# Two transformer blocks in one launch: a merged set of edits, and TensorE multiplying the identity while it waits for a norm

## The chip, the cores and the metric

The kernel runs on one core of a Trainium2 chip. A core has TensorE (matrix products into PSUM), VectorE, ScalarE, GpSimd and SyncE, which here issues all loads; 16 DMA engines move the data. The time is device time in microseconds (us) of the whole launch, median of several runs. In the profile PE is TensorE's matmuls, PEld its weight loads, DVE is VectorE, ACT ScalarE, POOL GpSimd, and SPq the queue of SyncE.

## What is computed

All is float32, with 256 tokens of width 1024. Cut to what matters:

```python
def first_block(x):                     # two layers
    for i in (0, 1):
        h = rms_norm(x, mix_pre_g[i])
        y = conformer_conv_module(h) if i == 0 else dilated_mixture_attention(h, k_sh, v_sh)
        x = x + rms_norm(y, mix_post_g[i])
        y = conv_ffn(rms_norm(x, ffn_pre_g[i]))          # 1024 -> 2 x 2816 -> 1024
        x = x + rms_norm(y, ffn_post_g[i])
        if i == 0:
            k_sh, v_sh = split(rms_norm(x, kv_norm_g) @ w_kv)
def second_block(x):
    u = modulate(rmsnorm(x, norm1_g), sh1, sc1)          # sh, sc, g from silu(c) @ ada_w
    x = x + g1 * token_mixer(u, uc)                      # mLSTM and differential attention
    u = modulate(rmsnorm(x, norm2_g), sh2, sc2)
    logits = u @ router_w + router_b                     # 32 experts, the best 4 of each token
    gate = softmax(top_k(logits, 4))
    y = sum over experts e of gate_e * (swiglu(u @ w1[e] + b1[e]) @ w2[e] + b2[e])
    x = x + g2 * y
    return rmsnorm(x, final_norm_g)
```

## The kernel before

**Layout.** Activations lie feature-major: eight chunks (`KT`) of 128 features by 256 tokens. Weights of the dense layers come in slabs of 1 MB (128 x 2048 floats) through a ring of five (`RING`), in the order of `LOADS`; slab `g` may be loaded when slab `g - 5` has been used (`slab_used`). SyncE issues them in one written-out order, and it also waits in that order, so that whatever stands behind a wait in its program is late with it.

**Dense stages.** `product` (L513) multiplies one slab by the eight chunks: 16 matmuls of 128x128 by 256, each two instructions in the trace, into one of three PSUM banks ("units"). `stage` (from `product`) runs the slabs of one matrix. The first product after a norm is the one with `wait_chunk`: it takes the chunks in the order in which the norm delivers them (L523); the others run at L534. A norm goes: ScalarE squares, TensorE multiplies by a constant mean matrix (`stat`, L574), ScalarE takes the root, VectorE the reciprocal, and VectorE or ScalarE scales the chunks. Before three of the products (`n2`, `n4`, `n7`) the norm's scale is applied later, so the product needs only the residual; the squares of these norms are summed by GpSimd (`presum`, L1306), and TensorE multiplies the sum (`presummed`, L590) after the first product. The residual is L1334 and L1337 of VectorE.

**Between the mixer and the experts.** SyncE stands at `wa`, the first matrix after attention, until the last head is done, and loads the router's weights and the experts' b2 into memory that attention used. After `wo` come the norm `n10`; 16 transposes of H into token-major `U2T` (L871); the router's products, 16 with 32 columns (L879); on VectorE the best four of each token in two passes, one for each half of the tokens (from L1685); products that count the tokens of each expert (L885 to L890); eight products of b2 and the gates (L900), copied to `YACC`; and `gather(0)` (L911), which picks the tokens of the first two experts.

**Experts.** A loop over 16 pairs of experts. Each pair has 24 slabs of 1 MB: 16 in `up` (L940 bias, L946), eight in `down` (L973). Within a pair stand also `scatter` (L922) of the pair before, which VectorE adds into `YACC` (L1770), the gather of the next pair (L911) and transposes (`hidden`). The slabs go round through 12 slots (`EXPERT_RING`): the five of the ring, three in `spare`, four in `arena`. Since 24 is a multiple of 12, one body serves every pair. A slab is loaded when the slab 12 places before it has been used (L503). The first five slots are loaded as the ring comes free, the other seven when the last product of `wo` is done. At the end stand one more scatter, X + g2 * YACC in eight operations (L1809), the last norm (L1015, L574, L1318, L1324) and one store of 1 MB (L507).

Of the kernel before, what the change touches and what calls it, by code (L numbers as in the profile page):

```python
# [19 lines left out]
P = 128  # L20
T = 256
D = 1024
KT = D // P
# [5 lines left out]
EXPERTS = 32  # L29
TOP_K = 4  # L30
CAP = 64
PAIRS = EXPERTS // 2
SLAB = 2048
RING = 5
EXPERT_RING = 12
# [151 lines left out]
def build(nc, d_x, d_ctx, d_par, d_con, d_mmask, d_rows, d_gatew, d_routerw, d_b1, d_b2, d_cond, d_dense, d_experts, d_out):  # L187
    ctx = ExitStack()
    with ctx:
# [6 lines left out]
        for kind, count, stages in (  # L196
                ("sq", KT, norms + ["hm", "do", "n10", "n11"]), ("sum", 1, norms + ["n10", "n11"]),
                ("root", 1, norms + ["n10", "n11"]), ("x", KT, ["n1", "n3", "n6", "n8", "n11"]),
# [105 lines left out]
        U2T = tiles(area(NB, 2048), 2)  # L304
        YACC = tiles(area(NB + 2048, 2048), KT)
        XGT = tiles(area(NB + 4096, 1024), KT)
        GL, LN, SGM = (tiles(area(NB + 5120 + 512 * i, 512), 2) for i in range(3))
        ACTT = tiles(area(NB + 6656, 1024), 8)
        YE = area(NB + 7680, 1024)
        SGT = area(NB + 8704, 256)  # L310
        SEL = tiles(area(NB + 8960, 256), 2)
        SELG = tiles(area(NB + 9216, 256), 2)
        NCOL = 4 * EXPERTS + 2
        POSA = tiles(area(NB + 9472, 2 * NCOL), 2)
        GATA = tiles(area(NB + 9472 + 2 * NCOL, 2 * NCOL), 2)
        MO = NB + 9472 + 4 * NCOL
# [4 lines left out]
        GTT = arena[0:EXPERTS, MO + 640:MO + 896]  # L321
        MORE = [spare[:, SLAB * i:SLAB * (i + 1)] for i in range(3)] + [area(NB + 11264 + SLAB * i, SLAB) for i in range(4)]
        B2 = arena[0:EXPERTS, NB + 19456:NB + 20480]
        ACTS = tiles(area(NB + 19456, 1024), 4)
# [14 lines left out]
        RW = area(NB + 20480, 256).rearrange("p (k n) -> p k n", k=KT)  # L339
# [4 lines left out]
        def expert_slab(j):  # L344

            q = j % EXPERT_RING
            return slab(DENSE_SLABS + q) if q < RING else MORE[q - RING]

        def slot_sem(j):
            q = j % EXPERT_RING  # L350
            return sem(f"slab{(DENSE_SLABS + q) % RING if q < RING else q}")
# [51 lines left out]
        def passes(eng, body, first=None):  # L403

            with eng.Fori(0 if first is None else first, PAIRS) as p:
                body(p)
            extra = extra_passes(eng)
            loaded[eng] = extra
            with eng.If(extra > 0):
                with eng.Fori(PAIRS, (extra + 1) * PAIRS) as n:  # L410
                    body(n)
# [38 lines left out]
        def _(sp):  # L450
# [3 lines left out]
            sp.dma_start(par[:, :], d_par).then_inc(sem("par_in"), 16)  # L454
            for g in range(DENSE_SLABS):
# [14 lines left out]
                if g == SLAB_AT["wa", 0]:  # L470
                    sp.wait_ge(sem("d_pv"), HEADS)
# [1408 lines left out]
```

## Time and profile before

| | |
|---|---|
| median of 3 runs | 2550.23 us (2549.61 to 2550.98) |
| the profiled execution, its own time | 2555.48 us |
| its span, first to last instruction | 2553.7 us |
| mean granted TensorE clock | 0.975 of full |
| PE busy, share | 2400.6 us, 94% |
| DVE, ACT, POOL busy | 752.9, 423.7, 17.0 us |
| read from HBM | 604.65 MB, 237 GB/s over the span |

Busy shares are averages over the span. The rows of slices show how they change: each digit is one fortieth of the span (63.8 us), in tenths of full. In brackets behind a row stands how long the engine had been idle before it, and what ended the idle time.

### The profile page before, as it was taken

How to read it: one execution, taken by the hardware profiler on the slowest of the kernel's cores; microseconds unless marked ns; L12 is line 12 of the kernel's file. 1: busy time of each engine (PE TensorE's matmuls, PEld its weight loads, DVE VectorE, ACT ScalarE, POOL GpSimd, SP SyncE). 2: the span in 40 equal slices, each digit the busy share in tenths (PEclk: the TensorE clock that was granted, in tenths of full speed). 3: DMA queues.
4: the chain of work that ended last, by engine and by line, in shares of the span. 5: the costliest groups of instructions: out<-in, count | busy, mean ns of one | idle time of the engine just before them, and what ended most of it. 6: DMA issues, size and time to landing. Idle time of an engine off the chain costs nothing.

```text
span 2553.7 us, 32904 instructions
## 1 busy us (share of the span) xinstructions
PE 2400.6 (94%) x13428; PEld 1806.2 (71%) x13428; DVE 752.9 (29%) x1781; ACT 423.7 (17%) x948; POOL 17.0 (1%) x25
## 2 busy tenths in 40 slices
PE   8799999999889998999998798999999999999997
PEld 7678888888778887888776586555555555555554
DVE  5834373210533312000345533222212211111212
ACT  3231102010331103000023512111111111111111
POOL 0000000000000000000000000000000000000000
PEclk9899999999999999899999997999999999999999
DMA  6134476654124443131120144999999999999996
GB/s 239 43 106 159 148 280 231 231 215 174 56 97 151 148 148 116 50 128 71 66 83 33 66 170 169 393 422 421 422 422 422 422 421 422 422 422 422 422 422 254
DMA packets 83841, 606.88 MB, mean 238 GB/s; under 512 B 9328, under 2 KB 9712, under 8 KB 10000
## 3 DMA queue, kind: packets, MB, share of 16 engines
q1 hardware_dynamic: 83760, 605.73, 59.9%
q8 instruction: 59, 0.97, 0.2%
q14 instruction: 22, 0.18, 0.0%
HBM read 604.65 MB, written 1.05 MB: 237 GB/s over the span
## 4 chain that ended last, share of the span: by engine, by line
PE 79%; DMA 10%; DVE 6%; ACT 3%; issue 1%; SPq 0%; ACTq 0%; DVEq 0%
PE bank L534 26%; PE bank L946 13%; DMA spare<-in_experts 9%; PE bank L531 8%; PE bank L973 6%; PE bank L605 5%; PE bank L523 4%; PE bank L911 3%; PE bank L548 2%; PE bank L940 2%; DVE arena L1436 2%; PE bank L922 1%; PE bank L685 1%; PE bank L616 1%; PE bank L574 1%
## 5 line engine op out<-in xcount | busy, mean ns | idle before, releaser
L534 PE MATMUL bank<-arena,ring 128*128 128x256 f32 x3296 | 717.2, 380 | 0.0
L534 PEld LDWEIGHTS bank<-arena,ring 128*128 128x128 f32 x3296 | 629.4, 191 | 84.4
L946 PE MATMUL bank<-ring,arena 128*64 128x256 f32 x2304 | 293.9, 383 | 18.2 <-DMA ring<-in_experts 10.3
L946 PEld LDWEIGHTS bank<-ring,arena 128*64 128x64 f32 x2304 | 175.2, 137 | 132.1 <-DMA ring<-in_experts 20.4
L1789 DVE TENSOR_SCALAR arena<-bank 128x256 f32<-128x256 f32 x64 | 27.2, 425 | 704.9 <-PE bank L946 704.9
L531 PE MATMUL bank<-ring,arena 128*128 128x256 f32 x896 | 196.1, 382 | 0.0
L531 PEld LDWEIGHTS bank<-ring,arena 128*128 128x128 f32 x896 | 171.7, 192 | 23.1
L946 PE MATMUL bank<-spare,arena 128*64 128x256 f32 x768 | 117.5, 383 | 7.9 <-DMA spare<-in_experts 7.9
L605 PE MATMUL bank<-arena,ring 128*128 128x256 f32 x576 | 124.6, 379 | 0.0
L523 PE MATMUL bank<-arena,ring 128*128 128x256 f32 x352 | 93.0, 431 | 29.2 <-ACT arena L1030 15.1
L605 PEld LDWEIGHTS bank<-arena,ring 128*128 128x128 f32 x576 | 109.7, 190 | 14.7
L946 PE MATMUL bank<-arena 128*64 128x256 f32 x1024 | 117.6, 383 | 0.0
L973 PE MATMUL bank<-spare,arena 128*64 128x512 f32 x384 | 113.3, 595 | 0.0
L973 PE MATMUL bank<-arena 128*64 128x512 f32 x512 | 113.1, 593 | 0.0
L523 PEld LDWEIGHTS bank<-arena,ring 128*128 128x128 f32 x352 | 76.8, 220 | 44.6 <-issue 31.8
L946 PEld LDWEIGHTS bank<-arena 128*64 128x64 f32 x1024 | 70.7, 137 | 44.6 <-issue 12.3
L1414 DVE SCALAR_TENSOR_TENSOR arena<-ring,arena 128x1024 f32<-128x1024 f32 x64 | 74.9, 1222 | 72.7 <-DMA ring<-in_dense 72.6
L946 PEld LDWEIGHTS bank<-spare,arena 128*64 128x64 f32 x768 | 69.2, 137 | 31.0 <-DMA spare<-in_experts 13.3
L1273 ACT ACTIVATE arena<-arena 128x256 f32<-128x256 f32 x64 | 26.7, 417 | 386.7 <-DVE arena L1789 377.7
L973 PEld LDWEIGHTS bank<-arena 128*64 128x64 f32 x512 | 44.2, 137 | 65.6 <-issue 65.6
L548 PE MATMUL bank<-arena,ring 128*128 128x256 f32 x384 | 88.9, 390 | 0.0
L1357 DVE SCALAR_TENSOR_TENSOR arena<-arena,par 128x254 f32<-128x254 f32 (+1 forms) x176 | 73.3, 479 | 51.0 <-ACT arena L1054 51.0
(260 smaller groups left out, 2146.3 us busy)
## 6 DMA issues: line engine op xcount, KB each, us to landing
ring<-in_dense SPq DMA_DIRECT2D x186, 1024.0 KB, 4.8
ring<-in_experts SPq DMA_DIRECT2D x160, 1024.0 KB, 22.4
arena<-in_experts SPq DMA_DIRECT2D x128, 1024.0 KB, 21.4
spare<-in_experts SPq DMA_DIRECT2D x96, 1024.0 KB, 21.8
con<-in_con SPq DMA_DIRECT2D x1, 1248.0 KB, 12.2
X<-in_x SPq DMA_DIRECT2D x1, 1024.0 KB, 5.0
arena<-in_cond SPq DMA_DIRECT2D x1, 1024.0 KB, 17.7
arena<-in_ctx SPq DMA_DIRECT2D x1, 1024.0 KB, 4.9
```

What stands on the lines that cost most here:

```text
L523: ins = nc.tensor.matmul(half_of(u, j), w[:, k, j * P:(j + 1) * P], src[:, k, :], start=(k == 0 and j == 0), stop=(k == KT - 1), skip_grou ...
L531: ins = nc.tensor.matmul(o, src[:, k, j * P:(j + 1) * P], w[:, k, :], start=(k == 0), stop=(k == KT - 1))
L534: ins = nc.tensor.matmul(o, w[:, k, j * P:(j + 1) * P], src[:, k, :], start=(k == 0), stop=(k == KT - 1))
L548: ins = nc.tensor.matmul(o, w[:, k, j * P:(j + 1) * P], H[:, k, :], start=(k == 0), stop=(k == KT - 1))
L605: ins = nc.tensor.matmul(banks[WORK + m // 2][:, (m % 2) * T:(m % 2 + 1) * T], w[:, kk, m * P:(m + 1) * P], F_ACT[:, k, :], start=(k == 0 ...
L911: ins = nc.tensor.matmul(banks[4 + b][:, (c % 4) * P:(c % 4 + 1) * P], U2T[:, t, c * P:(c + 1) * P], SEL[:, t, :], start=(t == 0), stop=(t ...
L940: nc.tensor.matmul(o, ONEH[:, e * CAP:(e + 1) * CAP], B1[:, i * T:(i + 1) * T], start=True, stop=False)
L946: ins = nc.tensor.matmul(o, XGT[:, k, e * CAP:(e + 1) * CAP], w[:, k, :], start=False, stop=(k == KT - 1))
L973: ins = nc.tensor.matmul(banks[2 + half][e * CAP:(e + 1) * CAP, :], ACTT[:, k, e * CAP:(e + 1) * CAP], w[:, kk, half * 512:(half + 1) * 51 ...
L1357: ins = V.scalar_tensor_tensor(o, F_U[j % 2][:, half, 0:T - back], par_col("ffn_dw", (layer * 3 + 2 - back) * 44 + c), o, ALU.mult, ALU.add)
L1414: V.scalar_tensor_tensor(JUNK[:, n % 3, :], w[:, j, :], 1.0, CSR[:, v, :], ALU.mult, ALU.mult, accum_out=MOD[:, 2 * i + j, v:v + 1]).then_ ...
L1436: ins = V.scalar_tensor_tensor(U[:, c + i, :], src, w, U[:, c + i, :], ALU.mult, ALU.add)
```

## The change

Two sets of edits are made together.

The first set ("the merge"):
- The sums of squares of `n2`, `n4`, `n7` are added by VectorE after the residual; GpSimd has no work left.
- The experts have 16 slots for 12. Since 24 is no multiple of 16, the loop body now holds two pairs (`odd` 0 and 1). The wait for attention moves from `wa`'s first slab to `wb`'s second; five expert slabs are loaded there, five more before `wo`'s first slab, each group behind waits of its own, five as the ring comes free and one after `wo`.
- The router multiplies with its weights stationary (eight products, 32 x 256 out), and the logits are turned by two transposes; the transposes of H are partly moved behind it. Both halves of the tokens are routed in one pass. The selection of the first pair's tokens comes directly after the counts.
- b2 times the gates is no product of its own: b2 is loaded into the first rows of `YE` and the gates are put into `SGT`, so that the first scatter of the loop does it. `YACC` is gone: VectorE adds g2 times the scattered bank to X directly, in two operations for each bank.
- At the end ScalarE squares each pair of chunks as it is added, and the output leaves in four stores.

The second set: `keep_busy`. In the first product after a norm, after the waits for slab and bank and before that for the first chunk, TensorE multiplies the identity by 256 columns of constants into the unit's own bank. Nobody reads it: the product then starts the bank anew. 6, 8, 10, 10, 10 and 7 such products stand before `cm_in`, `cm_out`, `ffn0_in`, `kv`, `ffn1_in` and `mq`.

```diff
-EXPERT_RING = 12
+EXPERT_RING = 16
...
-        MORE = [spare[:, SLAB * i:SLAB * (i + 1)] for i in range(3)] + [area(NB + 11264 + SLAB * i, SLAB) for i in range(4)]
+        MORE = [area(NB + at, SLAB) for at in (0, 2048, 4096, 17408, 19456, 13312, 15360)]
+        MORE += [spare[:, SLAB * i:SLAB * (i + 1)] for i in (0, 2, 1)]
+        LAST_SLOT = area(NB + 11264, SLAB)
...
-            with eng.Fori(0 if first is None else first, PAIRS) as p:
-                body(p)
+            with eng.Fori(0 if first is None else first, PAIRS // 2) as m:
+                for odd in range(2):
+                    body(m * 2, odd)
...
-                if g == SLAB_AT["wa", 0]:
+                if g == SLAB_AT["wb", 1]:
                     sp.wait_ge(sem("d_pv"), HEADS)
+                    for j in range(5):
+                        first_load(j)
+                if g == SLAB_AT["wo", 0]:
+                    sp.wait_ge(sem("b_out"), KT)
+                    for j in range(5, 7):
+                        first_load(j)
+                    sp.wait_ge(sem("a_out"), KT)
+                    first_load(7)
+                    sp.wait_ge(sem("do_root"), 4)
+                    first_load(8)
+                    units_read(sp, "wa")
+                    first_load(9)
                     sp.dma_start(RW, d_routerw).then_inc(sem("routerw_in"), 16)
-                    sp.dma_start(B2, d_b2).then_inc(sem("b2_in"), 16)
+                if g == SLAB_AT["wo", 2]:
+                    sp.wait_ge(sem("ye"), 1)
+                    sp.dma_start(YE[0:EXPERTS, :], d_b2).then_inc(sem("b2_in"), 16)
...
-            sp.wait_ge(sem("n11_h"), before("n11_h") + KT)
-            sp.dma_start(d_out, H).then_inc(sem("out_done"), 16)
-            sp.wait_ge(sem("out_done"), 16)
+            for c in range(0, KT, 2):
+                sp.wait_ge(sem("n11_h"), before("n11_h") + c + 2)
+                sp.dma_start(d_out[:, c:c + 2, :], H[:, c:c + 2, :]).then_inc(sem("out_done"), 16)
+            sp.wait_ge(sem("out_done"), 64)
...
-            def product(u, g, src, token_major=False, wait_chunk=None):
+            def keep_busy(u, count):
+
+                for _ in range(count):
+                    nc.tensor.matmul(half_of(u, 1), ident, C("ident", T), start=True, stop=True)
+
+            def product(u, g, src, token_major=False, wait_chunk=None, busy=0):
...
                 if wait_chunk:
+                    keep_busy(u, busy)
                     for k in range(KT):
...
-            stage("cm_in", H, "n0_h")
+            stage("cm_in", H, "n0_h", busy=6)
...
-            out_stage("cm_out", H, "ln_h", "n1")
-            stage("ffn0_in", H, "n2_h", count=1)
+            out_stage("cm_out", H, "ln_h", "n1", busy=8)
+            stage("ffn0_in", H, "n2_h", count=1, busy=10)
...
-            stage("kv", H, "n4_h", count=1)
+            stage("kv", H, "n4_h", count=1, busy=10)
...
-            stage("ffn1_in", H, "n7_h", count=1)
+            stage("ffn1_in", H, "n7_h", count=1, busy=10)
...
-            stage("mq", H, "n9_h")
+            stage("mq", H, "n9_h", busy=7)
...
             units_read(pe, "wo")
             pe.wait_ge(sem("routerw_in"), 16)
+            for k in range(KT):
+                pe.wait_ge(sem("n10_h"), before("n10_h") + k + 1)
+                ins = nc.tensor.matmul(banks[0][0:EXPERTS, 0:T], RW[:, k, :], H[:, k, :], start=(k == 0), stop=(k == KT - 1))
+            ins.then_inc(sem("logits_t"), 1)
...
+            turn_tokens(0)
+            pe.wait_ge(sem("lgt"), 1)
             for t in range(2):
+                ins = nc.tensor.transpose(banks[2][:, 32 * t:32 * t + 32], LGT[:, t * P:(t + 1) * P],
+                                          ident[0:EXPERTS, 0:EXPERTS])
             ins.then_inc(sem("logits"), 1)
+            for b in range(1, 4):
+                turn_tokens(b)
...
-            for c in range(KT):
-                ins = nc.tensor.matmul(acc(c), B2[:, c * P:(c + 1) * P], GTT, start=True, stop=True)
-                if c % 2:
-                    ins.then_inc(sem("b2_done"), 1)
...
-            for name in ("n2", "n4", "n7"):
-                for c in range(1, KT):
-                    pool.wait_ge(sem(name + "_sq"), before(name + "_sq") + c + 1)
-                    if c > 1:
-                        pool.wait_ge(sem(name + "_presum"), before(name + "_presum") + c - 1)
-                    nc.gpsimd.tensor_tensor(SQ[:, 0, :], SQ[:, 0, :], SQ[:, c, :], ALU.add).then_inc(sem(name + "_presum"), 1)
...
+            def presum(name):
+
+                for c in range(1, KT):
+                    dve.wait_ge(sem(name + "_sq"), before(name + "_sq") + c + 1)
+                    if c > 1:
+                        dve.wait_ge(sem(name + "_presum"), before(name + "_presum") + c - 1)
+                    V.tensor_tensor(SQ[:, 0, :], SQ[:, 0, :], SQ[:, c, :], ALU.add).then_inc(sem(name + "_presum"), 1)
...
-                    V.tensor_tensor(YACC[:, 2 * j:2 * j + 2, :], YACC[:, 2 * j:2 * j + 2, :],
-                                    tiles(banks[6 + j % 2][:, :], 2), ALU.add).then_inc(sem("scat_read"), 1)
+                    for c in (2 * j, 2 * j + 1):
+                        ins = V.scalar_tensor_tensor(X[:, c, :], banks[6 + j % 2][:, c % 2 * T:(c % 2 + 1) * T],
+                                                     MOD[:, 40 + c, 0:1], X[:, c, :], ALU.mult, ALU.add)
+                    ins.then_inc(sem("scat_read"), 1)
...
-            for c in range(KT):
-                V.scalar_tensor_tensor(X[:, c, :], YACC[:, c, :], MOD[:, 40 + c, 0:1], X[:, c, :], ALU.mult, ALU.add)\
-                 .then_inc(sem("n11_x"), 1)
```

## Rows read from the trace of the kernel before

**Rows 1.** The page's 40 slices: granted clock and DMA, in tenths.

```profile
PEclk9899999999999999899999997999999999999999
DMA  6134476654124443131120144999999999999996
```

**Rows 2.** Windows: length, busy us (instructions) by engine, clock, DMA share, GB/s.

```profile
1680.00:1760.00 80.00, 78.79 (x562) 45.11 (x560) 15.05 (x48) 9.11 (x17) 0.00 (x0) 1.00 1.01 422
...
1916.00:1976.00 60.00, 56.79 (x416) 32.52 (x414) 11.22 (x32) 6.54 (x12) 0.00 (x0) 1.00 1.01 422
```

**Rows 3.** Chain of waits in order of time, gathers: start, us, what.

```profile
1629.23 3.78 PE bank L911 x32
...
1857.30 3.78 PE bank L911 x32
...
1916.99 3.78 PE bank L911 x32
...
2513.76 3.78 PE bank L911 x32
```

**Rows 4.** Timeline of PE, first products after norms, and wa, wb: start, us, instruction.

```profile
16.76 10.06 PE L523 MATMUL bank<-arena,ring 128*128 128x256 f32 x32 [3.06 <-DVE arena L1324]
...
127.06 8.83 PE L523 MATMUL bank<-arena,ring 128*128 128x256 f32 x32 [3.54 <-ACT arena L1106]
...
165.64 9.02 PE L523 MATMUL bank<-arena,ring 128*128 128x256 f32 x32 [5.31 <-ACT arena L1030]
...
404.78 8.83 PE L523 MATMUL bank<-arena,ring 128*128 128x256 f32 x32 [4.56 <-ACT arena L1030]
...
996.23 10.13 PE L523 MATMUL bank<-arena,ring 128*128 128x256 f32 x32 [4.32 <-ACT arena L1152]
...
1462.48 8.83 PE L523 MATMUL bank<-arena,ring 128*128 128x256 f32 x32 [3.23 <-DMA ring<-in_dense]
...
1492.73 7.07 PE L523 MATMUL bank<-arena,ring 128*128 128x256 f32 x32
```

**Rows 5.** Timeline of all engines around the product at 165.64 us.

```profile
164.87 0.48 DVE L1334 SCALAR_TENSOR_TENSOR arena<-arena,par 128x256 f32<-128x256 f32 x1
...
168.81 0.95 DVE L1334 SCALAR_TENSOR_TENSOR arena<-arena,par 128x256 f32<-128x256 f32 x1
...
172.22 1.60 POOL L1306 TENSOR_TENSOR arena<-arena 128x256 f32<-128x256 f32 x2 [0.34 <-ACT arena L1031]
...
174.49 0.59 PE L590 MATMUL bank<-arena,con 128*128 128x256 f32 x2
```

**Rows 6.** Timeline of all engines from the norm n10 to the first gather.

```profile
1555.56 4.89 PE L871 MATMUL bank<-con,arena 128*128 128x128 f32 x16 [3.95 <-ACT arena L1152]
...
1560.24 6.88 PE L879 MATMUL bank<-arena 128*128 128x32 f32 x32
...
1567.22 0.22 DVE L1685 TENSOR_TENSOR arena<-bank,rows 128x64 f32<-128x64 f32 x1 [8.98 <-PE bank L879]
...
1570.90 0.63 PE L885 MATMUL bank<-arena,con 128*128 128x32 f32 x2 [3.79 <-DVE arena L1700]
...
1573.28 0.19 DVE L1713 TENSOR_REDUCE arena<-bank 128x1 f32<-128x32 f32 x1 [1.27 <-PE bank L890]
...
1583.54 6.61 PE L911 MATMUL bank<-arena 128*128 128x128 f32 x32 [0.78 <-DVE arena L1754]
```

**Rows 7.** Timelines of wo's second unit and of the tail.

```profile
1541.28 0.88 DVE L1675 SCALAR_TENSOR_TENSOR X<-bank,small,X 128x256 f32<-128x256 f32 x2 [6.03 <-PE bank L534]
...
2538.74 3.26 DVE L1809 SCALAR_TENSOR_TENSOR X<-arena,small,X 128x256 f32<-128x256 f32 x8
...
2549.43 0.36 SPq L507 DMA_DIRECT2D out<-arena  x1
```

**Rows 8.** DMA issues: count, KB each, median us to landing.

```profile
arena<-in_experts SPq DMA_DIRECT2D x128, 1024.0 KB, 21.4
...
arena<-in_routerw SPq DMA_DIRECT2D x1, 128.0 KB, 1.9
```

More of the change, by code:

```diff
@@ L409, in passes @@
             with eng.If(extra > 0):
-                with eng.Fori(PAIRS, (extra + 1) * PAIRS) as n:
-                    body(n)
+                with eng.Fori(PAIRS // 2, (extra + 1) * (PAIRS // 2)) as m:
+                    for odd in range(2):
+                        body(m * 2, odd)
         def total_pairs(eng):
@@ L536, in product, with stage @@
                 ins.then_inc(sem(f"unit{u % UNIT_BANKS}"), 1)
-            def stage(name, src, ready=None, token_major=False, first=0, count=None):
+            def stage(name, src, ready=None, token_major=False, first=0, count=None, busy=0):
                 n = SLABS_OF[name] if count is None else count
@@ L541, in stage @@
                     wait = (lambda k: pe.wait_ge(sem(ready), before(ready) + k + 1)) if ready and i == first else None
-                    product(FIRST_UNIT[name] + i, SLAB_AT[name, i], src, token_major, wait)
+                    product(FIRST_UNIT[name] + i, SLAB_AT[name, i], src, token_major, wait, busy)
             def half_product(o, g, j):
@@ L577, in stat, with out_stage @@
                     ins.then_inc(sem(name + "_sum"), 1)
-            def out_stage(name, src, ready, stat_name):
+            def out_stage(name, src, ready, stat_name, busy=0):
                 for i in range(4):
-                    stage(name, src, ready if i == 0 else None, first=i, count=1)
+                    stage(name, src, ready if i == 0 else None, first=i, count=1, busy=busy)
                     if i:
@@ L892, in _ @@
-            pe.wait_ge(sem("gate_w"), 2)
+            for b in range(1, 4):
+                turn_tokens(b)
+            pe.wait_ge(sem("chosen"), 1)
+            M0 = SR[0][:, 0:32]
+            nc.tensor.matmul(banks[1][:, 0:64], C("before"), SR[0], start=True, stop=False, skip_group_check=True)
+            for to in (32, 64):
+                nc.tensor.matmul(banks[1][:, to:to + 32], ones, M0, start=False, stop=to == 32, skip_group_check=True)
+            nc.tensor.matmul(banks[1][:, 64:96], ones, SR[0][:, 32:64], start=False, stop=True, skip_group_check=True)\
+                .then_inc(sem("places"), 1)
```

271 lines of the change are left out of this document (140 added, 131 removed).

## The prediction

> **What bounds the kernel now.** I read the page first. In the row of slices the DMA engines are at 9 from slice 26 (1596 us) on, and idle or half idle before; TensorE's clock is short of full in single slices, most in slice 25, where it is 7 [rows 1]. So there are two kernels in one: up to about 1590 us TensorE sets the pace, and its gaps are the loss; after that the experts' weights stream in.
>
> The windows say how full the stream is: 422 GB/s at a share of 1.01 in both, but TensorE 78.79 of 80 us busy in the early one and 56.79 of 60 in the later one [rows 2]. The chain of waits, in order of time, gives the periods. The gathers of the first five pairs are 57.02 us apart, (1857.30 - 1629.23) / 4; from the one at 1916.99 on they are (2513.76 - 1916.99) / 10 = 59.68 us apart [rows 3]. 59.68 / 24 slabs is 2.487 us a slab: the stream's rate. So 57.02 is TensorE's own pace, it lives on the twelve slabs fetched ahead for five pairs, and for eleven pairs the stream bounds: 11 x 2.66 = 29 us are lost to it.
>
> TensorE's timeline shows the rest. The first product after a norm waits 3.06, 3.54, 5.31, 4.56 and 4.32 us at five places (the sixth, at 745.93 us, repeats the third with 5.21) and then takes 10.06, 8.83, 9.02, 8.83 and 10.13 us, where the same 32 instructions take 7.07 at full clock [rows 4]. One more product, at 1462.48, waits 3.23 us for its weights, though nothing had moved before.
>
> **The change part by part.** I sum gains against the profiled execution (2555.48 us, span 2553.7); its time is 5.25 us above the median of the runs, 2550.23, and I take the differences over to the median unchanged.
>
> *Warm-ups.* Each is one 128x256 product: 7.07 / 16 = 0.44 us at full clock. 6, 8, 10, 10, 10 and 7 of them make 2.7, 3.5, 4.4, 4.4, 4.4 and 3.1 us, against gaps of 3.06, 3.54, 5.31, 4.56, 5.21 and 4.32 [rows 4]. All fit, the second and fourth with 0.04 and 0.16 us to spare. They lie in time in which TensorE has nothing; if its clock were already at 1.2 GHz they would take double and the cover would be gone: ten would be 8.8 us, 4.2 late in the fourth place. What they save is the slow part of the product: 10.06 - 7.07 = 3.0 at the first place, 1.7 at the second (8.83, less a little for the tight fit), 3.0 at the sixth. At the other three the product is not last, next point.
>
> *Presums to VectorE.* After those three products TensorE wants the sum of squares, which ends at 174.49 in the first of them [rows 5]. GpSimd adds it while VectorE runs the residual, and VectorE's same operation goes from 0.48 to 0.95 us beside it [rows 5]. Without GpSimd the residual ends near 164.5 + 8 x 0.73 = 170.1 us (0.73: one product and one addition, as at its start), then seven additions of about 0.45 end at 173.2, 0.5 after the product at full clock (165.64 + 7.07 = 172.7). The next product starts near 173.7 and not 174.9: 1.2, likewise 1.0 and 1.2 at the others. Without the warm-ups this term would be near nothing, as the product itself ends at 174.66. Six places: 3.0 + 1.7 + 1.2 + 1.0 + 1.2 + 3.0 = 11.1 us. All is TensorE's path (or feeds VectorE's convolution, which starts with the first units), so it should pass through. Bounds: 6 (clock regained in half of them) to 13.
>
> *The load queue before the experts.* SyncE waits for the last head of attention before it fetches wa; now that wait stands at wb's second slab, so wa is there. The 3.23 us go, except for the wait for VectorE's first gated chunk, for which I take 0.9; without that idle time the product (8.83) should keep its clock, 1.7 more [rows 4]: 4.0, bounds 2.3 and 4.0. Behind the moved wait stand five expert loads, and before wo five more: 5 x 2.487 = 12.4 us of stream. wb's second slab is wanted 33 us after wa starts and wo 52 us after; both lie well behind. At no cost.
>
> *Router.* Now 16 transposes, 16 products, routing, eight b2 products and four copies stand in a row: 1555.56, 1560.24, 1567.22 (logits), 1570.90 (chosen), 1583.54 (gather) [rows 6]. After: eight 256-column products at low clock, 0.88 each, end at 1562.6; a copy, four and two transposes, about 1.3: logits at 1563.9, 3.3 earlier. Thirteen routing instructions in one pass for twenty in two: 2.5 us for 3.6, 1.2 earlier. From chosen to gather 12.6 us now, of which 2.4 until the counts are there (1573.28) [rows 6]; after it are those 2.4 and additions and four selections (1.3), at the least 3.7; but the exponential, which VectorE waits for first, now stands behind twelve more transposes and four copies, so I take 4.5: 8.1 earlier, as b2 goes into the first scatter. Sum 12.6; bounds 9 (clock later back in the first products) and 16 (clock full in the router).
>
> *16 slots for 12.* Four more slabs lie ready when the first pair starts, and the stream has 368 to bring for 372: 4 x 2.487 = 9.9 us [rows 3]. It holds as long as the stream still bounds: TensorE has 29 us to spare, 9.9 go, and some 5 for the new scatter (two instructions of 0.88 us together where one addition stands now; I take 0.3 us a pair) [rows 7]: 14 left. All sixteen can have landed before the gather: the last is issued at the end of wo, more than 20 us ahead. Bounds 8 and 10.
>
> *Tail.* Eight scalings into X (3.26 us) go, and 0.4 comes in per two chunks: X is ready 2.9 earlier. The output goes out in four parts; now it is issued at 2549.43 and ends the span 4.3 later, while a 128 KB load lands in 1.9 [rows 7, 8], so 2.5 for the last 256 KB: 1.6 more. 4.5, less 0.3 for the last scatter. Bounds 3 and 6.
>
> Sum: 11.1 + 4.0 + 12.6 + 9.9 + 4.2 = 41.8 us, so 2550.2 - 41.8 = 2508.4 us. Bounds: 28 to 49.
>
> **Rivals.**
> *The loop turns too far back (slower).* A body is now two pairs. One pair is 830 TensorE instructions (416 and 414) [rows 2], two are 1660. If they don't fit where TensorE keeps them, each of the 7 turns back waits for a fetch. Nothing in the trace prices it; below nothing, above the 21.4 us of a slab in the full queue [rows 8]. 14 us are to spare, so the kernel would be slower from (41.8 + 14) / 7 = 8 us a turn; at 21.4 it would end at 2508 + 150 - 14 = 2644. Against it: for a body of 830 there is no lost time at a turn in the periods of the first five pairs, all 57.02 [rows 3].
> The Trainium skill (Runtime: NRT & Kernel Launch, Instruction fetch mechanics) gives TensorE room for 2048 instructions, and also says that a taken branch out of the present two pages of 256 forces a fetch. By the first the new body just fits; by the second the old one would already pay at each turn, which the equal periods do not show.
> *The warm-ups do not hold the clock, or are late.* Reading one matrix over again might not count as work. For it: the clock stayed low from 1556 us on while TensorE ran small matrices (the clock's slice 25 [rows 1]). Against: these are full 128x128 by 256, the same shape that regains it. Then 11.1 falls to about 1: 2518.
> *Expert loads in the way.* If SyncE's waits before wo (gated chunks, roots) end late, ten slabs queue ahead of the weights of wo, up to 12.4 us: 2521. The 52 us of cover speak against.
> *TensorE bounds the experts.* If the loop or scatter costs over 0.9 us a pair more, the slots' gain shrinks: 9.9 lost at most, 2518.
>
> **How the numbers follow.** Forecast 0.74 (2501 to 2515 its own range); warm-ups fail 0.08; loads in the way 0.05; TensorE bounds 0.07; loop turns 0.06, half of it above the present time. Eight in ten: 2499 to 2521, which leaves out the loop's case and the extremes of the sum. 0.2% (5 us) is about what a measurement of this kernel can tell; faster by more 0.96, within 0.01, slower 0.03.
>
> **What would show it.** Right: products after the norms at 7.1 us with the gaps filled; clock full there; no wait for in_dense at wa; logits to gather about 7 us; gathers at 57.0 to 57.4 us for eight or nine pairs and 59.68 after; the last load near 41 us earlier. Wrong: a gap at every second pair's start; a warm-up row at 0.88 each; an idle TensorE before wo; a router stretch that stays above 20 us from the end of wo.

## The result and the profile after

The changed kernel takes 2514.98 us (median of 4 runs, 2513.32 to 2517.58), the one before 2550.2 us: a ratio of 0.9863, interval 0.9846 to 0.988. That is 35 us less, where 2508.4 us (42 less) was forecast; the time lies in the range. Four more runs of the same kernel had a median of 2514.93 (2513.96 to 2519.58).

The profiled execution took 2513.32 us (span 2511.2). The page's slices, clock and DMA, against [rows 1]:

```profile
PEclk9999999999999999899999999999999999999999
DMA  6034475664224442132122173999999999999996
```

Slice 25, where the router stood at 7, is at 9 now. DMA is at 9 from slice 26 on, as before.

TensorE's timeline at places of [rows 4]; L543 is the identity product, L556 a stage's first product, L607 a norm's sum, L623 the sum over VectorE's additions. The six places with warm-ups are named here by the norm or the product behind it: n0 (`cm_in`), ln (`cm_out`), n2 (`ffn0_in`), kv, n7 (`ffn1_in`) and mq; nc is one more norm, whose sum stands shortly ahead of mq:

```profile
13.30 2.75 PE L543 MATMUL bank<-con 128*128 128x256 f32 x12
16.43 7.17 PE L556 MATMUL bank<-arena,ring 128*128 128x256 f32 x32 [0.38 <-DVE arena L1358]
...
123.40 7.17 PE L556 MATMUL bank<-arena,ring 128*128 128x256 f32 x32
...
160.23 7.17 PE L556 MATMUL bank<-arena,ring 128*128 128x256 f32 x32 [0.90 <-ACT arena L1066]
167.92 0.70 PE L623 MATMUL bank<-arena,con 128*128 128x256 f32 x2 [0.52 <-DVE arena L1380]
...
393.21 1.89 PE L607 MATMUL bank<-arena,con 128*128 128x256 f32 x8
397.34 6.27 PE L543 MATMUL bank<-con 128*128 128x256 f32 x20 [2.25 <-DMA ring<-in_dense]
403.45 7.07 PE L556 MATMUL bank<-arena,ring 128*128 128x256 f32 x32
...
979.13 6.47 PE L607 MATMUL bank<-arena,con 128*128 128x256 f32 x16 [3.54 <-ACT arena L1051]
...
990.08 3.19 PE L543 MATMUL bank<-con 128*128 128x256 f32 x14
994.39 7.17 PE L556 MATMUL bank<-arena,ring 128*128 128x256 f32 x32 [1.12 <-ACT arena L1188]
...
1449.39 7.14 PE L556 MATMUL bank<-arena,ring 128*128 128x256 f32 x32 [0.91 <-DVE arena L1684]
```

(The profile splits each f32 product in two records: x12 are the six of the code.) All seven products take 7.1 to 7.2 us now. But at 397.34 the twenty records of warm-up wait for a slab and take 6.27 us in place of the 4.48 they take elsewhere, and at 979.13 a norm's sum takes 6.47 us, where at full clock it takes 3.72.

The router, timeline of all engines, against [rows 6]; L607 is the sum of the norm n10:

```profile
1533.21 3.62 PE L607 MATMUL bank<-arena,con 128*128 128x256 f32 x16
...
1540.43 5.30 PE L903 MATMUL bank<-arena 128*32 128x256 f32 x16 [3.60 <-ACT arena L1188]
...
1546.66 0.23 DVE L1739 TENSOR_TENSOR arena<-bank,rows 128x64 f32<-128x64 f32 x1 [3.39 <-PE bank L917]
...
1548.75 1.28 ACT L1299 ACT_TABLE_LOAD   x1
...
1550.68 0.22 DVE L1761 TENSOR_TENSOR arena<-arena 128x64 f32<-128x64 f32 x1 [1.80 <-ACT arena L1299]
...
1552.91 6.31 PE L943 MATMUL bank<-arena 128*128 128x128 f32 x32 [0.63 <-DVE arena L1774]
...
1560.09 0.75 PE L974 MATMUL bank<-arena 32*64 32x256 f32 x4 [0.87 <-ACT arena L1306]
```

In the kernel before the same sum stands at

```profile
1547.99 3.62 PE L574 MATMUL bank<-arena,con 128*128 128x256 f32 x16
```

From the start of n10's sum (1533.21) to the first gather there are 19.70 us; before there were 35.55, to 1583.54 [rows 6]. The exponential is what VectorE waits for, as forecast: 1.80 us idle, and 1.28 us of ScalarE's time just ahead of the exponential is the load of its table.

The experts, gathers of pairs 1, 9, 10 and 16 on TensorE's timeline, against [rows 3]:

```profile
1598.42 1.83 PE L943 MATMUL bank<-arena 128*128 128x128 f32 x14
...
2056.05 3.84 PE L943 MATMUL bank<-arena 128*128 128x128 f32 x32
...
2115.00 2.16 PE L943 MATMUL bank<-arena 128*128 128x128 f32 x17
...
2473.39 2.83 PE L943 MATMUL bank<-arena 128*128 128x128 f32 x23
```

(2056.05 - 1598.42) / 8 = 57.20 us for eight pairs, then, after one of 58.95, (2473.39 - 2115.00) / 6 = 59.73: TensorE sets the pace for nine pairs now, for five before. A window from the first of these stretches, columns as in [rows 2]:

```profile
1820.00:1880.00 60.00, 58.98 (x440) 34.07 (x436) 12.61 (x38) 5.28 (x12) 0.00 (x0) 1.00 1.01 422
```

The tail, timeline of all engines, against [rows 7]:

```profile
2493.83 4.09 PE L954 MATMUL bank<-arena 128*128 128x256 f32 x16 [1.39 <-ACT arena L1329]
...
2497.10 1.74 DVE L1818 SCALAR_TENSOR_TENSOR X<-bank,small,X 128x256 f32<-128x256 f32 x4 [0.36 <-PE bank L954]
...
2498.89 3.72 PE L607 MATMUL bank<-arena,con 128*128 128x256 f32 x16 [0.97 <-DVE X L1818]
...
2506.30 2.71 SPq L534 DMA_DIRECT2D out<-arena  x4
```

**Stage by stage.** The lengths in us, each from the start of one named instruction to the next, in profiled executions of both kernels (two of each):

| stage | before | after |
|---|---|---|
| start to mq's second product | 1006.20, 1007.29 | 1001.40, 1002.39 |
| mixer, to the product for do (L886) | 450.3, 446.6 | 444.3, 444.4 |
| wa, wb, wo, to n10's sum | 91.5, 89.9 | 87.5, 87.5 |
| router, to the first gather | 35.55, 35.54 | 19.70, 19.70 |
| experts, first to last gather | 930.2, 927.3 | 920.5, 921.6 |
| tail | 40.0, 40.0 | 37.8, 37.7 |

The first columns differ by 42.5 us, which looks like the forecast's 41.8. It isn't: 6.0 of them are the mixer, whose instructions on TensorE, VectorE and ScalarE are the same in both kernels.

### The profile page after: what moved, and what is told of

Its sections match the earlier page's. It is cut to its first block, busy times and chain, and to the rows that moved or that the text cites. A ratio compares the mean times of both kernels' runs of the same rounds, so it can differ in the third digit from the quotient of the medians.

```text
span 2511.2 us, 32943 instructions
## 1 busy us (share of the span) xinstructions
PE 2391.6 (95%) x13498; PEld 1800.1 (72%) x13498; DVE 760.0 (30%) x1846; ACT 412.0 (16%) x941; POOL 0.2 (0%) x4
## 4 chain that ended last, share of the span: by engine, by line
PE 72%; SPq 15%; DVE 6%; ACT 3%; issue 2%; DMA 2%; DVEq 0%; ACTq 0%
PE bank L567 27%; SPq L529 15%; PE bank L980 10%; PE bank L564 8%; PE bank L638 5%; PE bank L1007 5%; PE bank L556 3%; DVE arena L1478 2%; PE bank L581 2%; PE bank L943 2%; PE bank L974 2%; PE bank L607 1%; DMA arena<-in_experts 1%; PE bank L718 1%; PE bank L649 1%
## 5 line engine op out<-in xcount | busy, mean ns | idle before, releaser
L567 PE MATMUL bank<-arena,ring 128*128 128x256 f32 x3296 | 716.3, 380 | 0.0
L980 PE MATMUL bank<-arena 128*64 128x256 f32 x2048 | 293.7, 383 | 6.8 <-DMA arena<-in_experts 4.4
L980 PEld LDWEIGHTS bank<-arena 128*64 128x64 f32 x2048 | 173.7, 137 | 96.8 <-issue 20.0
L980 PE MATMUL bank<-ring,arena 128*64 128x256 f32 x1280 | 176.3, 382 | 8.0 <-DMA ring<-in_experts 5.1
L980 PEld LDWEIGHTS bank<-ring,arena 128*64 128x64 f32 x1280 | 104.6, 137 | 75.7 <-issue 13.9
L1007 PE MATMUL bank<-arena 128*64 128x512 f32 x512 | 140.1, 594 | 3.0 <-ACT arena L1326 3.0
L638 PE MATMUL bank<-arena,ring 128*128 128x256 f32 x576 | 124.6, 380 | 0.0
L1007 PEld LDWEIGHTS bank<-arena 128*64 128x64 f32 x512 | 49.8, 137 | 66.3 <-issue 66.3
L581 PE MATMUL bank<-arena,ring 128*128 128x256 f32 x384 | 87.0, 384 | 0.0
L1090 ACT ACTIVATE arena<-arena,par 128x256 f32<-128x256 f32 x88 | 48.0, 592 | 229.8 <-DVE arena L1388 229.8
L974 PE MATMUL bank<-arena 32*64 32x256 f32 x512 | 83.1, 400 | 0.9 <-ACT arena L1306 0.9
```

Source lines behind the costliest of these rows:

```text
L567: ins = nc.tensor.matmul(o, w[:, k, j * P:(j + 1) * P], src[:, k, :], start=(k == 0), stop=(k == KT - 1))
L581: ins = nc.tensor.matmul(o, w[:, k, j * P:(j + 1) * P], H[:, k, :], start=(k == 0), stop=(k == KT - 1))
L638: ins = nc.tensor.matmul(banks[WORK + m // 2][:, (m % 2) * T:(m % 2 + 1) * T], w[:, kk, m * P:(m + 1) * P], F_ACT[:, k, :], start=(k == 0 ...
L974: nc.tensor.matmul(o, ONEH[:, e * CAP:(e + 1) * CAP], B1[:, i * T:(i + 1) * T], start=True, stop=False)
L980: ins = nc.tensor.matmul(o, XGT[:, k, e * CAP:(e + 1) * CAP], w[:, k, :], start=False, stop=(k == KT - 1))
L1007: ins = nc.tensor.matmul(banks[2 + half][e * CAP:(e + 1) * CAP, :], ACTT[:, k, e * CAP:(e + 1) * CAP], w[:, kk, half * 512:(half + 1) * 51 ...
```

## The experiments

Medians of the variants are of four to seven runs each. Over all sets of runs the kernel before had a median of 2550.5 us (31 runs, 2547.3 to 2554.7), and the kernel after, in two sets, 2514.9 (8 runs, 2513.3 to 2519.6). Those two are what the others stand against.

**Both kernels once more.** For the scatter of a stage between executions of one kernel; the second figures of the table are theirs.

> The kernel before, unchanged, profiled a second time. Theory: its first profile (2553.7 us span, own time 5.3 us above the median of the runs) had more of TensorE's time at the low clock by chance than a usual execution, and the place and length of the low stretches differ between executions of one program. Then the sum of low-clock time up to 1500 us differs from the first profile's by several us, and the own time is nearer to 2550. Rival: the low stretches are fixed by the program; then they lie where they lay, within 0.1 us, and the 5 us come from elsewhere.

> The changed kernel, unchanged, for a tighter interval and a second profile. Theory: 34 to 37 us below the kernel before, low-clock stretches at other places than in its first profile; the product after kv's warm-ups again starts about 8 us after the norm's last sum, since the warm-ups stand behind the wait for kv's first slab, which is issued only when the slabs of ffn0_out come free at once. Rival (the late slab was an accident of that execution): no wait for in_dense there.

The low stretches of the clock moved between the two executions of one kernel, as the first theory has it: in the kernel before, the product of `cm_out` (the norm ln) took 8.83 us in the first and 7.15 in the second, and the sum for nc 3.72 and 6.33. In the second execution of the kernel after, the warm-ups at kv waited for the slab again, 2.38 us, so that was no accident.

The router repeats to 0.01 us and the tail to 0.1. The mixer does not: 450.3 and 446.6 before, 444.3 and 444.4 after. Nor do the experts before, 930.2 and 927.3; why, no run shows. A row of TensorE's timeline and a window (length, busy, clock, DMA share, GB/s) in the mixer show what differs, here of the kernel after:

```profile
1259.64 1.96 PE L814 MATMUL bank<-arena 128*128 128x512 f32 x4 [3.28 <-DVE arena L1602]
```

```profile
1250.00:1275.00 25.00, 20.78 (x86) 1.00 0.24 84
```

and of an execution with a long mixer (450.5 us, the variant with warm-ups ahead of nc, below):

```profile
1261.09 2.74 PE L822 MATMUL bank<-arena 128*128 128x512 f32 x4 [3.28 <-DVE arena L1610]
```

```profile
1250.00:1275.00 25.00, 21.72 (x69) 0.80 0.12 42
```

After the same 3.28 us of idle time the clock stays at its upper level in one execution and falls to the lower one in the other. Over all fourteen profiled executions, of eleven kernels with the same mixer code, its length is 444.3 to 444.4 (six times), 446.6 to 446.7 (three times), or 449.7 to 450.5 (five times). The Trainium skill (TensorE: Matmul & The Clock Gate, What's actually happening) says that the place at which the clock changes depends on a phase that a kernel does not set, and differs from run to run; these rows agree, since the kernel before alone had both 450.3 and 446.6. Whether a mixer that long or short is only luck is not shown, though: the short length, 444.3, came in six of the ten executions with warm-ups (the kernel before with warm-ups among them) and in none of the four without. The warm-ups may make it likelier; no run decides.

**No warm-ups**, twice:

```diff
-            stage("cm_in", H, "n0_h", busy=6)
+            stage("cm_in", H, "n0_h")
...
-            stage("mq", H, "n9_h", busy=7)
+            stage("mq", H, "n9_h")
```

(all six places)

> The changed kernel with all six counts at 0, so the merge alone. Theory by the two traces: the warm-ups give 3.2, 2.1, 1.2, 1.1 and 3.0 us at five places and take 2 at kv, so this is 8 to 9 us slower than the changed kernel, about 2523.5; the products after norms take 8.8 to 10.1 us again. Rival (the clock is lost elsewhere anyway, so the slow time only moves): less than 4 us slower.

> The kernel after with all six warm-up counts at zero, a second time. Its first runs were 2512.8 to 2524.3 with a median of 2518.0, against 2514.9 for the kernel after: 3 us of warm-ups where the six places show about 5. If the warm-ups are worth what the places show, the two sets of runs together have a median of 2517 to 2520. If they are worth nothing, it comes to 2515.

Medians 2517.98 (0.9867, interval 0.9848 to 0.9887) and 2521.85 (0.9888, 0.9873 to 0.9903); all eight runs 2521.0, 2512.8 to 2525.2. So the merge without warm-ups brings 29.5 us and the warm-ups 6.1. The second figure is rough: against 2514.9 the two sets give 3.1 and 6.9. The expectation of 8 to 9 us missed. The first profile fell into low stretches like those of the first one of before (mixer 450.3), so those two can be compared directly: 2555.48 to 2524.31 us, 31.2. The second profiles of both (mixer 446.6 and 446.7) give 2548.35 to 2522.55, 25.8; the difference between the pairs lies mostly in the experts and wa. The timeline of the first at n2's product:

```profile
165.59 9.01 PE L556 MATMUL bank<-arena,ring 128*128 128x256 f32 x32 [5.31 <-ACT arena L1066]
174.43 0.59 PE L623 MATMUL bank<-arena,con 128*128 128x256 f32 x2
```

The sum starts with the end of the product, as before at 174.49 [rows 5]: the additions on VectorE bring nothing by themselves.

**The warm-ups on the kernel before**, the same six calls and helper, nothing else:

```diff
-            stage("kv", H, "n4_h", count=1)
+            stage("kv", H, "n4_h", count=1, busy=10)
```

> The kernel before with the same six sets of warm-ups and nothing of the merge. Theory by rows: 3.2, 2.1, 0.3, -2, 0.3 and 3.0 us, since without the presum on VectorE the products of n2, n4, n7 still wait for GpSimd: 5 to 7 us faster than before at equal luck with the clock. What the difference of x_no_warmups and the changed kernel says (3 us, within the scatter) would be 3 us here too.

2544.22 us, ratio 0.997 (0.9959 to 0.9981): 6.3 below the median of all runs of before, 7.6 below that of the eleven in its own set. By the other way round nearly the same price, 6 to 8, and not 11.1. At kv its timeline differs from that of the kernel after:

```profile
397.68 4.58 PE L516 MATMUL bank<-con 128*128 128x256 f32 x20 [2.18 <-DMA ring<-in_dense]
```

The ten warm-ups wait for the slab as long, but the clock does not fall, and they take 4.58 us and not 6.27. From the last sum to the next product it is 15.83 us, only 0.3 more than without warm-ups, where 2 more were expected. So the late start by itself costs little; what costs is the fall of the clock, and that came in all seven other profiled executions with this order.

**Warm-ups ahead of the wait for the slab.** In `product`:

```diff
-                slab_loaded(pe, g)
                 if u >= UNIT_BANKS:
                     unit_half(pe, u - UNIT_BANKS, 2)
+                keep_busy(u, busy if wait_chunk else 0)
+                slab_loaded(pe, g)
                 if wait_chunk:
-                    keep_busy(u, busy)
```

> The changed kernel with the warm-ups in front of the wait for the slab instead of behind it. Theory: at kv they start 2.25 us earlier, keep the clock, and the product starts with the first chunk, near 4.6 us after the last sum: 3 to 4 us faster than the changed kernel. Rival (the slab is late anyway and the product waits for it): within 1 us of it.

Timeline at kv, where the kernel after had 397.34 and 403.45:

```profile
393.52 1.89 PE L607 MATMUL bank<-arena,con 128*128 128x256 f32 x8
395.25 4.48 PE L543 MATMUL bank<-con 128*128 128x256 f32 x20
399.98 7.14 PE L556 MATMUL bank<-arena,ring 128*128 128x256 f32 x32 [0.24 <-ACT arena L1066]
...
408.09 3.18 PE L567 MATMUL bank<-arena,ring 128*128 128x256 f32 x14
```

The reader sees the warm-ups follow the sum directly, at full clock, and the product start with its first chunk. From the last sum to the next product it is 408.09 - 393.52 = 14.57 us; after 410.79 - 393.21 = 17.58, before 15.55. The place is repaired: 3.0 us. The median is 2515.67 (0.9861, 0.9844 to 0.9878) all the same, though 3 to 4 us less were expected. In its profile the mixer took 449.7 us, 5.3 more than in that of after, which would hide them; the other three runs have no profile. 3 us are less than what runs of one kernel differ by, and four runs don't show them.

**Presums back on GpSimd**, warm-ups kept:

```diff
+        @block.gpsimd
+        def _(pool):
+            for name in ("n2", "n4", "n7"):
...
-            presum("n2")
```

> The changed kernel with the three presums back on GpSimd and the warm-ups kept. Theory: after the products of n2, n4 and n7 TensorE waits for the presum until about 9 us after the product's start, 1.1 us later than with VectorE at the first and third place, less at kv, where the product itself starts late: 2 to 3.5 us slower. Rival (GpSimd's sum is as fast as VectorE's once the product is early): no difference at the presum's row.

Timeline of all engines at n2:

```profile
162.97 0.95 DVE L1379 SCALAR_TENSOR_TENSOR arena<-arena,par 128x256 f32<-128x256 f32 x1
...
165.39 4.41 PE L556 MATMUL bank<-arena,ring 128*128 128x256 f32 x16 [0.21 <-ACT arena L1066]
...
168.13 1.60 POOL L1351 TENSOR_TENSOR arena<-arena 128x256 f32<-128x256 f32 x2 [0.34 <-ACT arena L1067]
```

From the last sum to the next product 16.24 us, against 15.60 in the kernel after and 16.75 before: of the 1.15 us that n2 gained, 0.64 are VectorE's additions, and that only with the warm-ups there. At n7 it is the same, 15.87 and 15.24 us, and at kv nothing, 17.56 and 17.58: 1.3 us in all, where 2 to 3.5 were expected. Median 2515.04 (0.9851, 0.9836 to 0.9866): not to be seen in the time. The Trainium skill (SBUF — State Buffer, Who interferes with whom) says that VectorE and GpSimd share a port under a lock, so that the one that comes second waits; the trace agrees: VectorE's operation takes 0.95 us beside GpSimd's and 0.48 throughout in the kernel after, where GpSimd is idle.

**Twelve slots in the new loop**:

```diff
-EXPERT_RING = 16
+EXPERT_RING = 12
...
-            for r in range(RING):
+            for r in range(2):
                 slab_used(sp, DENSE_SLABS + r - RING)
                 first_load(len(MORE) + r)
             unit_ready(sp, FIRST_UNIT["wo"] + 3)
-            first_load(EXPERT_RING - 1)
```

> The changed kernel with 12 expert slots again, ten from the merge's own places and two in the ring; all else stays, also the loop body of two pairs. Theory: the gathers run at 57.2 us for about five pairs and at 59.7 from then on, and the last gather comes 9.4 to 10 us later relative to the first: 9.9 us slower, about 2525. Rival (the gain of the experts' stretch is the early start alone, or the body of two pairs costs time that the slots pay back): less than 5 us slower, or another period than 57.2.

Chain of waits in order of time, gathers of pairs 4 to 6 and 16:

```profile
1775.53 3.78 PE bank L942 x32
...
1833.02 3.78 PE bank L942 x32
...
1892.76 3.78 PE bank L942 x32
...
2490.18 3.78 PE bank L942 x32
```

57.5, 59.7 and so on to the end, (2490.18 - 1892.76) / 10 = 59.74: as before, from the gather of pair 5 on the stream bounds. First to last gather 931.7 us, 11.3 more than in the first profile of after; the eight executions with sixteen slots and the same router have 920.0 to 922.3, so 9.4 to 11.7 more. Median 2526.86 (0.9898, 0.9883 to 0.9913), 11.9 more. The four slots are worth 9 to 12 us in this loop.

**No wait for VectorE ahead of the last norm's sum**:

```diff
             scatter(n_end)
-            pe.wait_ge(sem("scat_read"), n_end * 4 + 6)
             stat("n11", 0, mean)
```

(the sum's own waits for its squares stay)

> The changed kernel without TensorE's wait for the last scatter's four additions in front of the last norm's sum; each of its eight products already waits for its own square, which ScalarE makes after the addition, so the wait orders nothing else. Theory: the sum overlaps with the additions as in the kernel before and ends 1.9 to 3 us earlier after the last product of the experts. Rival (the additions bound the tail): within 0.5 us in the rows of the tail. The total should move by the same 2 us, which the scatter of the runs may hide.

```profile
2495.22 4.09 PE L954 MATMUL bank<-arena 128*128 128x256 f32 x16 [1.34 <-ACT arena L1328]
...
2499.14 3.62 PE L607 MATMUL bank<-arena,con 128*128 128x256 f32 x16
```

On its timeline the sum follows the scatter without a gap and ends 8.9 us after the last down product, not 10.2; the tail is 36.5 us, not 37.8. That is less than the 1.9 to 3 expected. The median, 2516.54 (0.9865, 0.985 to 0.988), doesn't show the 1.3.

**Warm-ups ahead of nc's sum**:

```diff
             ffn_out(1, "n8")
+            u = FIRST_UNIT["mq"]
+            unit_half(pe, u - UNIT_BANKS, 2)
+            keep_busy(u, 7)
             stat("nc", 1, mean)
```

> The kernel after with seven more identity products ahead of the norm sum for nc (3.54 us of idle time stand there), into the next mq unit's bank. Theory one, the gain at mq was eaten because this gap lowers the clock for nc's sum: the sum takes 3.7 instead of 6.5 us, the stretch from its start to mq's second product is 2 to 3 us shorter than 22.3, and the median falls to about 2512.5. Theory two, the clock stays low there for another reason: the sum still takes 6.5 us and nothing changes. Theory three, the sum gets shorter and the wait for the next norm longer by the same, because VectorE is late anyway: 22.3 stays.

```profile
976.07 3.19 PE L543 MATMUL bank<-con 128*128 128x256 f32 x14
979.80 3.72 PE L612 MATMUL bank<-arena,con 128*128 128x256 f32 x16 [0.54 <-ACT arena L1059]
...
992.54 7.17 PE L561 MATMUL bank<-arena,ring 128*128 128x256 f32 x32 [1.35 <-ACT arena L1196]
```

The sum takes 3.72 us and not 6.47; from its start to mq's second product it is 19.75 us, after it was 22.27. Theory one holds for the place: 2.5 us. The median, 2514.49 (0.985, 0.9835 to 0.9865; single runs from 2508.53 to 2518.83), shows nothing, and the profiled run is the one with the mixer of 450.5 us above.

**Warm-ups in the router**, seven ahead of its products and three between the counts and the gather:

```diff
             units_read(pe, "wo")
+            busy_in(banks[0][:, 0:T], 7)
...
+            pe.wait_ge(sem("u2_out"), 4)
+            busy_in(banks[4][:, 0:T], 3)
             pe.wait_ge(sem("gate_w"), 1)
```

> The kernel after with seven identity products ahead of the router's eight products and three more between the token counts and the first gather. If TensorE's low clock in the router is on the way: router products 3.7 instead of 5.3 us, the gather about 4 instead of 6.3, the stretch from the sum n10 to the first gather 18 instead of 19.7 us, first up product 3 to 4 us earlier, and the experts gain it only in part, since the stream bounds the last seven pairs: the slabs come no sooner, so the last gather moves by 0 to 1 us and the time stays at 2514 to 2515. If the low clock there is not on the way either, the stretches themselves don't move.

```profile
1540.52 3.61 PE L909 MATMUL bank<-arena 128*32 128x256 f32 x16 [0.58 <-ACT arena L1196]
...
1551.32 3.81 PE L951 MATMUL bank<-arena 128*128 128x128 f32 x32 [0.84 <-DVE arena L1782]
1555.99 0.75 PE L982 MATMUL bank<-arena 32*64 32x256 f32 x4 [0.86 <-ACT arena L1314]
```

Products 3.61 for 5.30 us, gather 3.81 for 6.31, first up product 22.68 us after n10's sum starts and not 26.88: 4.2 earlier. All as expected, but not what I expected of the time: the last gather came 3.7 us earlier (936.5 us after that start, not 940.2, and not the 939.7 to 942.0 of the eight executions without these warm-ups), and the median is 2510.33 (0.9841, 0.9826 to 0.9856), 4.6 below after. The stream did not eat it. The windows of the kernel after show why:

```profile
1533.00:1560.00 27.00, 19.41 (x94) 14.40 (x92) 14.45 (x62) 11.56 (x23) 0.00 (x0) 0.81 0.20 78
1560.00:1570.00 10.00, 9.91 (x84) 5.74 (x86) 1.18 (x4) 0.80 (x1) 0.00 (x0) 1.00 0.44 167
1570.00:1580.00 10.00, 9.37 (x73) 5.85 (x69) 3.32 (x9) 1.31 (x3) 0.00 (x0) 1.00 1.01 388
```

The share is 0.20 until the first up product at 1560.09 (from 1545 to 1560 the stream moves 0 to 2 GB/s) and full ten microseconds later: the slots are filled, and the stream stands until the first of them has been read. Its start hangs on TensorE, and with it its end.

**All repairs together**: slab order, nc, router and tail.

> All the repairs together: warm-ups ahead of the wait for the slab, warm-ups ahead of nc's sum, warm-ups in the router, and no wait for the last addition ahead of the last norm's sum. By the places: kv 3.0, nc and mq 2 to 3, router 0 to 1 at the end of the stream, tail 1.2: 6 to 8 us, 2507 to 2509. If low stretches of the clock merely move from one place to another, as they did in the mixer, the median stays within 2 us of 2515.

2506.22 us (5 runs, 2502.04 to 2509.20), ratio 0.9827 (0.9814 to 0.9841): 8.7 below the kernel after, and the fastest here. The profiled execution, the fastest of its five as that of after is of its four, has the same short mixer as that of after (444.4, 444.3 us), so the two can be set against each other: 11.3 us. In it kv gains 3.0, nc and mq 2.5, n10's sum to the last gather 4.9 (1.3 more than with the router's warm-ups alone, about what executions of one kernel differ by there), the tail 1.3.

## Why the prediction was nearly right, point by point

What bounds the kernel held: two kernels in one, TensorE's gaps first, the stream after. Of the forecast 41.8 us, 35.6 came, all runs of the one against all of the other.

- **Warm-ups and presums: 11.1 forecast, 6.1 measured** (4.8 in the profiles, to mq's second product). This is the term that failed. Four of the six places held: n0 3.2 for 3.0, ln 1.7 for 1.7, n2 1.15 for 1.2, n7 1.15 for 1.2, each against the first profile of before; against the second ln gains 0.1 and n2 2.0, so single places are luck in part. kv *lost* 2.0 where 1.0 was to be gained. The step was "against gaps of 3.06, 3.54, 5.31, 4.56, 5.21 and 4.32. All fit": it took all of kv's gap as wait for the norm. But the first 2.25 us of it are also a wait for the slab, and the warm-ups stand behind that. They started 2.25 us after TensorE had fallen idle, 0.3 us later the granted clock fell to its lower level until 401.0, and they took 6.27 us for 4.48: from 397.34 to 403.6, although the first chunk was there near 399.7. The row of before named only the later of two waits, ScalarE [rows 4]. Shown by the experiment with the other order (3.0 back); the kernel before with warm-ups shows that without the fall of the clock only 0.3 are lost.
- **mq: 3.0 forecast, 0.4 to 1.6 measured.** The step "3.0 at the sixth" looked at the product alone. It does take 7.17 us for 10.13, but nc's sum ahead of it takes 6.47, behind 3.54 us of idle time that nobody fills. In the profiles without warm-ups the cost falls on the product alone (sum 3.72, product 10.14, 22.8 us in all) or on both (sum 6.40, product 8.83, 24.0); with them it falls on the sum (22.3). The sum stands ahead of the warm-ups at mq, so these cannot have slowed it: it took 5.3 to 6.6 us in all eight executions with warm-ups at mq alone, and 3.7 (twice) or 6.3 to 6.4 (twice) in the four without any. Only with nc's gap filled too does it go (19.75, shown).
- **VectorE's additions:** worth nothing without the warm-ups, as forecast (16.75 us both ways), and 0.64 of the 1.15 with them. Right, though two numbers of the working were off by little: 164.5 + 8 x 0.73 is 170.3 and not 170.1, and 174.49 [rows 5] is where TensorE multiplies the sum, which GpSimd had ended at 172.22 + 1.60 = 173.8.
- **wa: 4.0 forecast, 4.0 measured** against the profile that the sum used, with an idle time of 0.91 for the 0.9 taken; 2.4 against the second profile of before, where the product took 7.14 us already, behind 2.09 of idle time. The ten loads ahead of wo cost nothing: 87.5 us with no wait for a slab. Their cover was even larger than the 33 and 52 us of the working: wb's second slab is wanted 35.5 us after wa starts, and wo's first 56.2.
- **Router: 12.6 forecast, 15.85 measured**, the same to 0.1 us in every execution with this router and no warm-ups in it, at the upper bound of 16. It is the length of a stage; no run has the router's edits alone. The step mis-sized was "eight 256-column products at low clock, 0.88 each, end at 1562.6": they took 5.30 us and not 7.0, and the logits came 13.45 us after n10's sum began (1546.66 - 1533.21), where 15.9 was forecast (2.5 of the difference). The gather followed in 6.25 us for 7.0 (0.8). The low clock that I carried over from before stood under transposes and narrow products that are gone; that they had caused it is likely, but no run took them alone.
- **Slots: 9.9 forecast, 9.7 measured** in the profile that the sum used (930.15 to 920.48), 5.7 in the second pair, and 9.4 to 11.7 by the variant with twelve slots. The mechanism was right. TensorE's own pace rose by 0.18 us a pair, 0.3 was taken.
- **Tail: 4.2 forecast, 2.2 measured.** The last scatter and the additions ended 2.9 us earlier, as worked out, and the four stores brought 1.8 where 1.6 stood (by the prediction's own numbers, 4.3 less 2.5, it should have been 1.8). What failed is "X is ready 2.9 earlier", taken as gain in full: the norm's sum now stands behind the scatter on TensorE and behind a wait for VectorE's last addition, so its end moved by 0.6 only. 1.3 of it come back without that wait (shown in the rows of the tail, not in the median).
- **"I take the differences over to the median unchanged"** failed, though not by the 5.25 us it spoke of. The profiled execution of before had a mixer of 450.3 us, at the long end of three lengths; that of after 444.3. Had I judged by the two profiles alone, 42.5 us would have confirmed 41.8, with 6 of them from a stage that nobody changed. The account: 5.0 too much at the warm-ups, 3.2 too little at the router, 0.2 too much at the slots and 2.0 in the tail make 4.0 of the 6.2 that are missing. Up to 1.6 at wa and up to 4 at the slots (second profile of before) could hold the rest; what of it is the clock's luck stays open. That the total came within 7 us of the forecast owes something to luck: the error at the warm-ups and that at the router go opposite ways.

**The rivals.** *The loop turns too far back:* no. (A pair has 410 matmuls and 410 weight loads in the trace, 820; the 416 and 414 of the prediction are those of a window of 60 us.) The eight periods with a body of two pairs are 57.20 us each, turns inside or not; a fetch at each turn would lengthen every second one. By the Trainium skill (Runtime: NRT & Kernel Launch, Instruction fetch mechanics) a taken branch out of the present two pages must fetch first; no cost of such a fetch shows in these periods. *The warm-ups do not hold the clock, or are late:* the products behind them ran at full clock in all six places; late they were in one, kv, where the clock fell under them. This rival was right in one place of six, and the place would have been found by asking of each gap which wait ends first as well as which ends last. *Expert loads in the way, TensorE bounds the experts:* no.

## What to carry to other kernels

Work that fills a wait must stand ahead of every wait that belongs to the same gap: a row names the wait that ended last, so list the others before you put ten instructions behind one of them. A product that takes less time is not yet a gain: at mq the product lost its slow clock and the sum ahead of it, behind a gap of its own, had one. So fill all gaps of a chain, or price the chain and not the product. When two profiles are compared, compare first a stage whose code is the same in both: if it moved, that much of the difference is not the price of an edit, and effects below it need the stage's own rows, since medians of four runs do not show them.

## What the runs showed of the hardware

- The same code ran in one of three lengths, near 444.3, 446.6 or 450.3 us, by where TensorE's clock fell; and whole runs of one kernel scatter by 6 us or more (2513.3 to 2519.6 after, 2547.3 to 2554.7 before). That the one makes much of the other is likely; only the profiled executions show stages.
- Identity products whose result nobody reads hold the clock: over the router's 23 us (1533 to 1556) it was granted at 1.00 with ten of them, against 0.81 over the corresponding 27 us without.
- A weight stream that has filled its slots stops until the first slot is read (0 to 2 GB/s from 1545 to 1560 us). What is gained on TensorE before the loop then brings the end of the loop forward, though the stream bounds its second half: 3.7 of 4.2 us arrived at the last gather.
- Ten identity products behind 2.2 to 2.4 us of waiting for a slab took 6.27 us in seven profiled executions and 4.58 in one; ahead of that wait they took 4.48.
